# Storing split weights in two halves, and feeding the matmuls four columns of each half in turn

## What is computed

```python
h = h + stick_breaking_mixer(rmsnorm(h, sb_norm[0]), sb_w_qkv[0], sb_w_o[0])   # 16 heads of 128, causal
h = h + swiglu_ffn(rmsnorm(h, ffn_norm[0]), ffn_w_gate_up[0], ffn_w_down[0])   # 2048 -> 2 x 5632 -> 2048
h = h + chunked_gmlp_mixer(rmsnorm(h, gm_norm[0]), gm_w_in[0], gm_v_norm[0], gm_w_s[0], gm_b_s[0], gm_w_o[0])
h = h + swiglu_ffn(rmsnorm(h, ffn_norm[1]), ffn_w_gate_up[1], ffn_w_down[1])
out = rmsnorm(h, final_norm)

def swiglu_ffn(h, w_gate_up, w_down):
    gate, up = jnp.split(h @ w_gate_up, 2, axis=-1)
    return (jax.nn.silu(gate) * up) @ w_down
```

## Time and profile before

| | |
|---|---|
| time, median of 2 runs | 2097.84 us (2097.83 to 2097.85) |
| the profiled execution, its span | 2097.8 us |
| TensorE matmuls busy | 2088.2 us |
| VectorE busy | 1430.7 us |
| ScalarE busy | 1013.1 us |
| moved by DMA | 402.47 MB, mean 192 GB/s |
| clock granted to TensorE, mean | 0.999 |

### The profile page before, as it was taken

One profiled execution on the slowest core, in us unless ns is written; L12 is line 12 of the kernel. 1 busy time (PEld: TensorE's weight loads), 2 busy tenths in 40 slices (PEclk: granted clock), 3 DMA queues, 4 the chain that ended last, 5 costly groups with the idle time before them and its releaser, 6 DMA issues.

```text
span 2097.8 us, 27159 instructions
## 1 busy us (share of the span) xinstructions
PE 2088.2 (100%) x9281; PEld 1729.4 (82%) x9281; DVE 1430.7 (68%) x1822; ACT 1013.1 (48%) x1285; POOL 16.4 (1%) x30
## 2 busy tenths in 40 slices
PE   9999999999999999999999999999999999999998
PEld 7888888888888888888888888888888888888887
DVE  6787777867666676665557887877666676664444
ACT  6577765544444444444445444554444444444443
POOL 1000000000000000000000000000000000000000
PEclk9999999999999999999999999999999999999999
DMA  8555554666666666555566665566666666655554
GB/s 264 179 179 170 181 189 167 198 196 192 191 190 198 191 193 195 192 191 196 194 192 209 190 200 183 190 190 201 192 189 198 192 193 194 190 194 198 192 191 150
DMA packets 207419, 402.47 MB, mean 192 GB/s; under 512 B 12336, under 2 KB 13056, under 8 KB 206976
## 3 DMA queue, kind: packets, MB, share of 16 engines
q1 hardware_dynamic: 206496, 398.11, 61.1%
q0 software_dynamic: 688, 3.18, 0.4%
q10 hardware_dynamic: 176, 0.40, 0.1%
HBM read 399.55 MB, written 2.10 MB: 191 GB/s over the span
## 4 chain that ended last, share of the span: by engine, by line
PE 99%; issue 0%; DMA 0%; DVE 0%; ACT 0%; POOLq 0%; POOL 0%; DVEq 0%; SPq 0%
PE acc L1085 64%; PE acc L1091 32%; PE tp L1156 0%; PE tp L1176 0%; PE acc L1106 0%; PE acc L1107 0%; PE acc L1108 0%; PE tp L1302 0%; DMA h<-in_x 0%; PE tp L1116 0%; PE acc L1345 0%; PE acc L1344 0%; PE acc L1343 0%; PE acc L1143 0%; PE tp L1136 0%
## 5 line engine op out<-in xcount | busy, mean ns | idle before, releaser
L654 DVE TENSOR_TENSOR w_lo<-raw,w_hi 128x1024 fp32r<-128x1024 f32 x750 | 916.0, 1224 | 584.9 <-ACT w_hi L348 581.1
L348 ACT ACTIVATE w_hi<-raw 128x1024 fp32r<-128x1024 f32 x750 | 792.9, 1060 | 922.4 <-PE acc L1091 917.2
L1085 PE MATMUL acc<-w_hi,xT 128*128 128x512 f32 x4032 | 998.7, 390 | 0.0
L1085 PEld LDWEIGHTS acc<-w_hi,xT 128*128 128x128 f32 x4032 | 756.0, 188 | 155.9
L1091 PE MATMUL acc<-w_lo,xT 128*128 128x512 f32 x2016 | 539.2, 389 | 0.0
L1091 PEld LDWEIGHTS acc<-w_lo,xT 128*128 128x128 f32 x2016 | 378.6, 188 | 78.5
L1085 PE MATMUL acc<-w_hi,hid_hi 128*128 128x512 f32 x944 | 368.7, 391 | 0.0
L1085 PE MATMUL acc<-w_hi,hid_lo 128*128 128x512 f32 x944 | 367.6, 389 | 0.0
L1091 PE MATMUL acc<-w_lo,hid_hi 128*128 128x512 f32 x944 | 252.5, 389 | 0.0
L1091 PEld LDWEIGHTS acc<-w_lo,hid_hi 128*128 128x128 f32 x944 | 177.3, 188 | 36.7
L1085 PEld LDWEIGHTS acc<-w_hi,hid_hi 128*128 128x128 f32 x944 | 177.3, 188 | 36.8
(11 more groups left out here) (115 smaller groups left out, 477.6 us busy)
## 6 DMA issues: line engine op xcount, KB each, us to landing
raw<-in_ffn_w_gate_up SPq DMA_DIRECT2D x352, 512.0 KB, 4.5
raw<-in_ffn_w_down SPq DMA_DIRECT2D x176, 512.0 KB, 3.6
raw<-in_sb_w_qkv SPq DMA_DIRECT2D x95, 512.0 KB, 4.3
raw<-in_gm_w_in SPq DMA_DIRECT2D x64, 512.0 KB, 4.4
raw<-in_sb_w_o SPq DMA_DIRECT2D x32, 512.0 KB, 4.1
raw<-in_gm_w_o SPq DMA_DIRECT2D x32, 512.0 KB, 4.0
h<-in_x SPq DMA_DIRECT2D x3, 512.0 KB, 7.6
gain_bc<-in_gm_v_norm POOLq DMA_DIRECT2D x1, 1024.0 KB, 6.1
```

What stands on the lines that cost most here:

```text
L348: nc.scalar.activation(w_hi[:, p % RING], raw[:, p % RING], ACT.Copy).then_inc(hi_ready, 1)
L654: nc.vector.tensor_tensor(w_lo[:, p % RING], raw[:, p % RING], w_hi[:, p % RING].bitcast(f32), ALU.subtract).then_inc(lo_ready, 1)
L1085: nc.tensor.matmul(acc_at(chunk, r), part[:, kt, rs], w_hi[:, p % RING, k], start=(kt == 0 and part is hi), stop=False)
```

## The change

A line is 16 bytes here, 4 columns of float32. Each slot of `w_hi` and `w_lo` now has two halves ("bays"): of every tile, columns 0 to 255 lie in the first and 256 to 511 in the second, which begins BAY = 544 columns, 136 lines, further (8 modulo 16). A slot takes 2 x 544 + 8 = 1096 columns, 274 lines (2 modulo 16), so the four slots begin at 0, 2, 4 and 6 lines modulo 16, counted from the first. The splits write the same values through a view with one more dimension. The matmuls read four columns of the first half, four of the second, and so on upwards, and write to PSUM in the same order, so every sum ends where it did before. `raw` stays as it is, and so does the order of all instructions. To make room, `stop` and `below` move into the region, into a part that nothing else uses while attention runs; `region` is now aligned with `w_hi`'s start modulo 256 bytes.

```diff
+        BAY = KP * CH // 2 + 32
+        SLOT = 2 * BAY + 8
+        def ring_of_halves(name):
+            bays = sb(name, [P, RING, SLOT], f32r)[:, :, 0:2 * BAY].rearrange("p s (h m) -> p s h m", h=2)
+            return bays[:, :, :, 0:KP * CH // 2].rearrange("p s h (k n) -> p s k h n", k=KP)
-        w_hi = sb("w_hi", [P, RING, KP, CH], f32r)
-        w_lo = sb("w_lo", [P, RING, KP, CH], f32r)
+        w_hi = ring_of_halves("w_hi")
+        w_lo = ring_of_halves("w_lo")
+        W0 = nc.lookup_mloc(raw).addr + RING * KP * CH * 4
...
-        below = sb("below", [P, P])
-        stop = sb("stop", [P, 3 * P])
...
-        assert (R0 - nc.lookup_mloc(w_hi).addr) % CH == 0
+        assert (R0 - W0) % (CH // 2) == 0
...
+        stop = at("stop", HB + FREE + 2 * CB, [P, ZW])
+        below = at("below", HB + FREE + 2 * CB + ZB, [P, P])
...
+        def in_halves(piece):
+            return piece.rearrange("p k (h n) -> p k h n", h=2)
...
-                nc.scalar.activation(w_hi[:, p % RING], raw[:, p % RING], ACT.Copy).then_inc(hi_ready, 1)
+                nc.scalar.activation(w_hi[:, p % RING], in_halves(raw[:, p % RING]), ACT.Copy).then_inc(hi_ready, 1)
...
-                nc.vector.tensor_tensor(w_lo[:, p % RING], raw[:, p % RING], w_hi[:, p % RING].bitcast(f32),
+                nc.vector.tensor_tensor(w_lo[:, p % RING], in_halves(raw[:, p % RING]), w_hi[:, p % RING].bitcast(f32),
...
+            def by_turns(w, slot, k):
+                return w[:, slot, k].rearrange("p h (c e) -> p c h e", e=LINE)
+            def acc_by_turns(chunk, rt):
+                columns = acc_at(chunk, rt)
+                return columns.rearrange("p (h c e) -> p c h e", h=2, e=LINE)
...
-                                nc.tensor.matmul(acc_at(chunk, r), part[:, kt, rs], w_hi[:, p % RING, k],
+                                nc.tensor.matmul(acc_by_turns(chunk, r), part[:, kt, rs], by_turns(w_hi, p % RING, k),
```

More of the change, by code:

```diff
@@ L45, in hybrid_trunk @@
     KP = 2
+    LINE = 4
     PD = KD // KP
@@ L106, in hybrid_trunk @@
         used_up_to = nc.lookup_mloc(moments).addr + 32
-        lead_in = sb("lead_in", [P, (nc.lookup_mloc(w_hi).addr - used_up_to) % CH // 4])
+        lead_in = sb("lead_in", [P, (W0 - used_up_to) % (CH // 2) // 4])
         region = sb("region", [P, 2 * KF * S])
         R0 = nc.lookup_mloc(region).addr
-        assert (R0 - nc.lookup_mloc(w_hi).addr) % CH == 0
+        assert (R0 - W0) % (CH // 2) == 0
         HB = KF * S * 4
@@ L370, in split_half @@
                 ks = slice(n * KP // 2, (n + 1) * KP // 2)
-                nc.scalar.activation(w_hi[:, p, ks], raw[:, p, ks], ACT.Copy).then_inc(done, 1)
+                nc.scalar.activation(w_hi[:, p, ks], in_halves(raw[:, p, ks]), ACT.Copy).then_inc(done, 1)
             def squares(m, c, src):
@@ L680, in split_half @@
                 dve.wait_ge(ready, seen)
-                nc.vector.tensor_tensor(w_lo[:, p, ks], raw[:, p, ks], w_hi[:, p, ks].bitcast(f32),
+                nc.vector.tensor_tensor(w_lo[:, p, ks], in_halves(raw[:, p, ks]), w_hi[:, p, ks].bitcast(f32),
                                         ALU.subtract).then_inc(done, 1)
@@ L1090, in piece @@
                         for r in range(RT):
-                            last = nc.tensor.matmul(acc_at(chunk, r), hi[:, kt, r * P:(r + 1) * P],
-                                                    w_lo[:, p % RING, k], start=False, stop=(kt == K - 1))
+                            last = nc.tensor.matmul(acc_by_turns(chunk, r), hi[:, kt, r * P:(r + 1) * P],
+                                                    by_turns(w_lo, p % RING, k), start=False, stop=(kt == K - 1))
                     last.then_inc(used, 1)
@@ L1104, in piece @@
                         rs = slice(r * P, (r + 1) * P)
[L1105 to L1108, removed]
+                        dst = acc_by_turns(chunk, r)
+                        nc.tensor.matmul(dst, hi[:, kt, rs], by_turns(w_hi, p % RING, k), start=(kt == 0), stop=False)
+                        nc.tensor.matmul(dst, hi[:, kt, rs], by_turns(w_lo, p % RING, k), start=False, stop=False)
+                        last = nc.tensor.matmul(dst, lo[:, kt, rs], by_turns(w_hi, p % RING, k), start=False,
                                                 stop=(kt == K - 1))
@@ L1336, in _ @@
                 rs = slice(r * P, (r + 1) * P)
-                dst = acc_at(1, r)
+                dst = acc_by_turns(1, r)
                 for t in range(ROWWISE, 2 * PF):
@@ L1342, in _ @@
                         kt = (t - PF) * KP + k
-                        nc.tensor.matmul(dst, hid_hi[:, kt, rs], w_hi[:, t % RING, k], start=False, stop=False)
-                        nc.tensor.matmul(dst, hid_hi[:, kt, rs], w_lo[:, t % RING, k], start=False, stop=False)
-                        last = nc.tensor.matmul(dst, hid_lo[:, kt, rs], w_hi[:, t % RING, k], start=False,
+                        nc.tensor.matmul(dst, hid_hi[:, kt, rs], by_turns(w_hi, t % RING, k), start=False, stop=False)
+                        nc.tensor.matmul(dst, hid_hi[:, kt, rs], by_turns(w_lo, t % RING, k), start=False, stop=False)
+                        last = nc.tensor.matmul(dst, hid_lo[:, kt, rs], by_turns(w_hi, t % RING, k), start=False,
                                                 stop=(kt == KF - 1))
```

## The result

| | before | after |
|---|---|---|
| median | 2097.84 us | 2241.95 us (2241.77 to 2242.14, 2 runs) |
| profiled execution, its span | 2097.8 us | 2240.4 us |

The change makes the kernel slower, by a ratio of 1.0687 (95% interval 1.0656 to 1.0718), 144 us. The forecast was 2008 us with a range up to 2152.

The account below looks back on a forecast made before the run. The prediction took TensorE's matmuls, 226.7 ns from start to start, to bound the kernel. Fewer read meetings gave 90 us, every other part nothing: 2097.8 - 90 = 2008 us, range 1978 to 2152.

Parts of the forecast that it names:

- What bounds the kernel: TensorE is the whole chain: 9024 matmuls at 226.7 ns from start to start, 2045.7 us of 2097.8.
- the 13.3 ns: Each matmul's excess over 213.3 ns for 512 columns, 120 us in all, taken as operand reading from memory.
- Part (1): Matmul operands: moving reads by turns meet the stationary read less; 10 ns a matmul, 90 us gained, bounds -120 us to nothing.
- The one witness: Early starts 232.5 ns apart, 6 more than in step, read as a trace that the two reads' relative position counts.
- the signs: Expected in the changed profile: chain stays PE, all-idle starts tighten, four slots differ if position decides, splits keep their times.
- four periods that were named: Time per ring piece: 2.56 to 2.65 us if right, 2.72 unchanged, about 2.79 positions worse, over 3 patterns costly.
- Part (2): PSUM output written by turns of four columns: taken as costing nothing, bounded at 53 ns a matmul.
- Part (3): Splits on ScalarE and VectorE, output in four runs of 256: 0 to some 0.2 us a piece, hidden.
- Part (4): Moving stop and below into the region, surrounded only by attention's scratch: no wait added or removed, costs nothing.
- Worse positions: Rival for the operand reads: meetings recur on every run, 5.8 ns a matmul, +52 us, 2150 us; chance 0.12.
- Broken patterns cost: Rival for reads or PSUM: each 16-byte change of place costs a cycle, 53 ns a matmul, 2579 us; chance 0.10.
- The rival that nothing happens: The excess belongs to taking on weight tiles or to total bytes, not address order; 2098 us, chance 0.36.

Follow-up runs that it names:

- one_phase: Changed kernel with SLOT = 2 * BAY, so all ring slots begin at the same address modulo 256 bytes; 2217.45 us.
- near_halves: Memory layout of the kernel before, moving read and output both by turns of four columns, halves 64 lines apart; 2307.05 us.
- region_64: Kernel before with 64 bytes more padding ahead of the region, so hid_hi and hid_lo tiles lie 4 lines further; 2116.78 us.
- phases_only: Kernel before with each w_hi and w_lo slot 8 columns longer, so slots stand at four phases, reads in a row; 2149.82 us.
- streams: Matmuls alone, weight load on one line, then other turns and steps of the moving read; on one line: 231 ns in a row, 242 by turns 136 lines apart.
- patterns: Matmuls alone, trunk left out, 24 of each pattern: plain 226.7 ns, read by turns 240.4, output by turns 227.9.
- out_turns: Changed kernel with the old ring and reads in a row, so only the output is written by turns of four; 2097.28 us.
- phases: Matmuls alone, 32 of each pattern, mainly shifting the stationary or moving tile by lines: 226.8 ns plain, 233.2 with the stationary tile 2 lines further.

## Why the prediction was wrong

**What bounds the kernel.** Right, and it held through every run: each time was 2098 plus 9018 times what the distance gained. The count and the 226.7 ns carried `one_phase`, `near_halves`, `region_64` and `phases_only` to within 4 us. That the 13.3 ns are reading was right for 8 of them (a read on one line takes 218.7); the other 5.4 stay open.

**Part (1) is the step that failed.** Its term was 10 ns less a matmul, 90 us; measured were 16 ns more, 144 us. It failed in three ways. It took for the cause of the 13.3 ns a meeting of the moving read with the weight load, of which turns would rid it; the moving read is slow by its own order, and by turns it is slower, 240.0 against 226.7 at equal phase, 120 us (`one_phase`), and stays so when the load touches one line only (`streams`). It bounded the edit at "-120 us, and at worst nothing", though no row excluded a loss: the reading order had no row at all, and only the rivals, not the step, had a price for one. And it counted four phases as a remedy for three slots of four. Before stood at a best phase already, so that the others could only lose: 52 us with reads in a row (`phases_only`), 24.5 us on top of turns (2241.95 - 2217.45). The two do not add up (120 + 52 would be 172, the change lost 144), since by turns the phases are worth only some 3 ns.

The one witness, the 232.5 ns from 11.49 to 12.42 us, was misread. It was taken for matmuls whose loads are out of step, but only the load at 11.26 is. The next starts with the matmul at 11.49, and those at 11.73, 11.96 and 12.20 with theirs:

```profile
11.49 0.19 PEld L1108 LDWEIGHTS acc<-w_hi,xT 128*128 128x128 f32 x1
```

By address all was in step there too. `patterns` has such distances with TensorE alone: in its first pattern (L71), tiles in step, the starts after the clock has risen lie 229, 233, 236, 224, 231, 235, 229, 233 and 231 ns apart, and then 226.7. So the row showed matmuls that settle, as far as the runs tell, and not that something was left to gain. That reads out of phase also take 233 is not shown to have to do with it.

Nor did the signs help. The four slots did differ, by 0.03 us a piece, but they would under a loss too; and "wrong if 13.3 ns has nothing to do with where the runs lie" did not come true, since it has, though not to this edit's gain. A piece of 2.90 to 2.93 us fits none of the four periods that were named.

The Trainium skill, "TensorE: Matmul & The Clock Gate", section "Part 2: What happens when you issue a matmul", says that loading the next weights takes no read bandwidth from the running matmul. By it the step had nothing to gain, which was nearer than 90 us; literally it does not hold here, since the same moving read goes from 226.8 to 233.2 ns when only the stationary tile shifts by two lines. Its 215.7 ns for 512 columns agrees: the bf16 pattern (L137) has (5.35 - 0.38) / 23 = 216.1 ns, its first matmul included.

**Part (2)** was right: turns in PSUM cost nothing (2097.28 us). The Trainium skill, "PSUM — Partial Sum Buffer", section "Specifications (TRN2)", says that any non-contiguous pattern slows matmuls significantly; here output by turns of 4 (L83) and even of 2 columns (L107) has rows of 5.63 us for the plain 5.60, settling included, and the whole kernel shows nothing.

**Part (3)** was right in what counts: +10 ns on ScalarE's split and none on VectorE's, both hidden. **Part (4)** too: `out_turns` has the moves of `stop` and `below` in it and loses nothing.

**The rivals.** Slower had 0.22. "Worse positions" is right that position costs, but not that it is what makes turns slow. That its 5.8 ns and 2150 us are those of `phases_only` (52.6 us, 2149.82) is luck: they were taken from the misread row. "Broken patterns cost", at 53 ns, has the other mechanism on the reading side, but priced by the break; what was seen goes by the order of lines and stays at some 13.5 ns from 31 breaks (L108 of `streams`) to 127. The change did both, and its time lies between their two. The rival that nothing happens fell with the change.

**What stays open:** which division of the memory makes steps of 3 and 9 lines fast, of 5, 6, 10 and 16 slow and turns the same for 4, 8 and 16 columns. That it repeats modulo 16 lines is shown; why is not. The Trainium skill, "SBUF — State Buffer", section "Door 1: The DMA port swizzle", says in its box on cachelines that a 16-byte line needs two or more hits for full bandwidth and that each access that crosses to a new line pays a penalty. The 8 ns between one line over and over and a read in a row agree with a penalty; but all patterns of whole lines here have four hits in each line and as many crossings, and take from 226 to 320 ns: the order of the lines matters as well.

## What to carry to other kernels

When one engine is the whole chain, measure the distance between its starts, and price a new access pattern by running that pattern alone, 24 or 32 times in a row: it takes one small kernel, and its nanoseconds carried over to the whole kernel within 0.2%. For fp32r matmuls of 512 columns on this chip, read the moving operand in a row and keep its tiles and the stationary ones at the same address modulo 256 bytes; padding that looks idle may be what holds this. Where no row shows an edit's kind of access, its bound has a loss in it.

## What the runs showed of the hardware

- Moving reads of fp32r, 512 columns, all at the higher clock: 218.7 ns on one line, 226.7 in a row and in step, mostly 233 out of step, 240 to 251 by turns of 4 to 16 columns, up to 320 for every 6th line.
- The place of the stationary tile against the moving one counts modulo 16 lines of 16 bytes: 0, 1 and 15 lines further are free, the others cost 3 to 8 ns (`phases`). The moving tile 1 line further cost 5, and one phase came at 229 or 233 ns, depending on the run.
- The output's order in PSUM, in runs of 4 or 2 columns, is free.
- Settling is seen: after a change of pattern up to ten matmuls take 224 to 239 ns before the distance is steady. The odd starts at the beginning of the kernel before look like it.
